# The gates of a scan in whole blocks of four products, woven four times into the projections

## The reference

```
gate_a = sigmoid(blockdiag(xr) @ wa[d] + ba[d])
gate_x = sigmoid(blockdiag(xr) @ wx[d] + bx[d])
log_a  = -8 * gate_a * softplus(-lam[d])
a, u   = exp(log_a), sqrt(-expm1(2 * log_a)) * gate_x * xr
h      = forward scan of (a[0], u[0]) + backward scan of (a[1], u[1])
y      = h * gelu(xg)
```

## Time and profile before

| | us |
|---|---|
| median of 3 runs (lowest, highest) | 1549.49 (1547.18, 1549.74) |
| the profiled execution | 1548.46 |
| its span, first to last instruction | 1546.6 |
| PE busy | 1457.9 |
| DVE busy | 1025.9 |
| ACT busy | 740.9 |
| POOL busy | 445.8 |

### The profile page before, as it was taken

The page is one execution under the profiler, slowest core; times in us unless marked ns, Lnnn a source line. Parts: engine busy times, 40 slices in busy tenths (PEclk is TensorE's granted clock), DMA queues, the critical chain, the costliest instruction groups (busy, mean ns, idle before and its releaser), DMA issues.

```text
span 1546.6 us, 16079 instructions
## 1 busy us (share of the span) xinstructions
PE 1457.9 (94%) x5958; PEld 1023.3 (66%) x5958; DVE 1025.9 (66%) x1032; ACT 740.9 (48%) x716; POOL 445.8 (29%) x225
## 2 busy tenths in 40 slices
PE   6999999999999999999999933999999999999997
PEld 3444487857675444555568832888888888888774
DVE  4533144473864655565545575998999999998896
ACT  3301001064633124455524431777777777777773
POOL 0031000000021007798963440222222233322204
PEclk9999999999999999999999965999999999999998
DMA  9311040030013000000223276999999999999994
GB/s 318 139 55 55 0 139 1 1 119 28 28 28 61 0 7 21 1 28 28 68 84 123 95 267 237 352 367 371 377 378 377 378 378 378 378 374 371 378 380 191
DMA packets 152887, 284.48 MB, mean 184 GB/s; under 512 B 25300, under 2 KB 35874, under 8 KB 152835
## 3 DMA queue, kind: packets, MB, share of 16 engines
q1 hardware_dynamic: 147219, 263.32, 47.8%
q0 software_dynamic: 4464, 16.25, 4.0%
q10 hardware_dynamic: 1152, 4.19, 0.7%
HBM read 259.10 MB, written 24.64 MB: 183 GB/s over the span
## 4 chain that ended last, share of the span: by engine, by line
PE 84%; DVE 6%; DMA 4%; ACT 2%; issue 2%; POOL 1%; SPq 0%; POOLq 0%; DVEq 0%; ACTq 0%
PE psum L1707 10%; PE psum L1709 10%; PE psum L1708 10%; PE psum L1249 7%; PE psum L1227 5%; PE psum L1480 4%; PE psum L1338 4%; PE psum L1209 4%; DMA arena<-in_exp_w_down 3%; PE psum L1542 3%; PE psum L1449 3%; PE psum L1174 2%; PE psum L1618 2%; PE psum L1620 2%; PE psum L1530 2%; PE psum L1619 2%
## 5 line engine op out<-in xcount | busy, mean ns | idle before, releaser
L2241 DVE TENSOR_TENSOR split_at<-arena,split_at 128x2048 fp32r<-128x2048 f32 x188 | 428.0, 2290 | 61.6 <-ACT split_at L1090 60.1
L1090 ACT ACTIVATE split_at<-arena 128x2048 fp32r<-128x2048 f32 x192 | 367.8, 1916 | 68.4 <-PE psum L1709 54.3
L1707 PE MATMUL psum<-split_at,split_at 128*128 128x512 f32 x768 | 306.4, 399 | 1.4 <-DVE split_at L2247 1.4
L1709 PE MATMUL psum<-split_at,split_at 128*128 128x512 f32 x768 | 300.6, 391 | 0.0
L1708 PE MATMUL psum<-split_at,split_at 128*128 128x512 f32 x768 | 300.0, 391 | 0.0
L1709 PEld LDWEIGHTS psum<-split_at,split_at 128*128 128x128 f32 x768 | 144.8, 189 | 31.3
L1707 PEld LDWEIGHTS psum<-split_at,split_at 128*128 128x128 f32 x768 | 145.0, 189 | 29.8 <-DVE split_at L2247 1.8
L1708 PEld LDWEIGHTS psum<-split_at,split_at 128*128 128x128 f32 x768 | 145.2, 189 | 28.4
L628 POOL TENSOR_TENSOR arena<-arena 128x1024 f32<-128x1024 f32 x48 | 114.1, 2376 | 122.1 <-ACT arena L972 119.6
L685 POOL COPY arena<-arena 128x1 uint32 (+1 forms) x14 | 28.3, 2020 | 360.7 <-DVE arena L2275 360.7
L2052 DVE TENSOR_REDUCE arena<-psum 128x1 f32<-128x1024 f32 x64 | 78.1, 1224 | 68.1 <-PE psum L1449 67.4
(11 more groups left out here) (313 smaller groups left out, 2477.9 us busy)
## 6 DMA issues: line engine op xcount, KB each, us to landing
arena<-in_exp_w_gate SPq DMA_DIRECT2D x64, 1024.0 KB, 14.3
arena<-in_exp_w_up SPq DMA_DIRECT2D x64, 1024.0 KB, 14.6
arena<-in_exp_w_down SPq DMA_DIRECT2D x64, 1024.0 KB, 14.3
arena<-in_w_in SPq DMA_DIRECT2D x9, 1024.0 KB, 7.9
arena<-in_x SPq DMA_DIRECT2D x8, 512.0 KB, 6.5
xhat_scratch<-arena SPq DMA_DIRECT2D x8, 512.0 KB, 10.0
arena<-in_w_out SPq DMA_DIRECT2D x8, 512.0 KB, 3.6
arena<-xhat_scratch SPq DMA_DIRECT2D x8, 512.0 KB, 5.0
```

What stands on the lines that cost most here:

```text
L1090: a(flat(wsplit[c % WS][0]), wraw[:, c], ACT.Copy).then_inc(s_whi, 1)
L1707: mm(bank(out_bank), src[0][:, k, :], whi[:, k % 4, :], start=(k == 0), stop=False)
L1709: ins = mm(bank(out_bank), src[1][:, k, :], whi[:, k % 4, :], start=False, stop=(k == KT - 1))
L2241: tt(flat(lo), wraw[:, c], flat(hi), ALU.subtract).then_inc(s_wlo, 1)
```

## The change

PE's `gates(q)` now computes both token halves in one block of four products: half 0 goes to banks 0 and 1 as before, half 1 to banks 2 and 3. It waits once, until ACT has read both halves of the block before. ACT reads half `j` from banks `2j` and `2j + 1` and always both halves in a row. The block stands at four places instead of eight: behind three units of `I_KV`, behind all of `I_KV`, behind all of `I_KV + 1`, and (block 3) behind nine units of `I_CQ + 1` and the wait for the rotated key, where its first half stood before. Block 2 thus lies whole ahead of `I_CQ`, where its halves lay behind 9 and behind 18 units of it. `sum_squares(0)`, which still follows 18 units of `I_CQ`, gets a wait for ACT's reads of block 2, because it writes banks 2 and 3. On ACT, the second half of block 2 moves ahead of the root of `ckv`, and the second half of block 3 ahead of the squares of `I_CQ + 1`.

```diff
@@ ACT
-            def gates(q, js=(0, 1)):
+            def gates(q):
...
-                for j in js:
+                for j in range(2):
                     act.wait_ge(s_gmm, 2 * q + j + 1)
                     h = slice(HALF * j, HALF * j + HALF)
-                    a(lx_[:, h], bank(1), ACT.Sigmoid, bias=par[:, C_BX + q:C_BX + q + 1])
-                    a(lt_[:, h], bank(0), ACT.Sigmoid, bias=par[:, C_BA + q:C_BA + q + 1]).then_inc(s_gact, 1)
+                    a(lx_[:, h], bank(2 * j + 1), ACT.Sigmoid, bias=par[:, C_BX + q:C_BX + q + 1])
+                    a(lt_[:, h], bank(2 * j), ACT.Sigmoid, bias=par[:, C_BA + q:C_BA + q + 1]).then_inc(s_gact, 1)
...
-            gates(2, (0,))
+            gates(2)
             rms_root(rb, 1, KVL)
-            gates(2, (1,))
             w_high(I_CQ + 2)
             squares(I_CQ, 2)
             w_high(I_CQ + 3)
             gate_rates(2)
-            gates(3, (0,))
+            gates(3)
             squares(I_CQ + 1, 3)
             w_high(I_CQ + 4)
-            gates(3, (1,))
             gate_rates(3)
@@ PE
-            def gates(q, j):
+            def gates(q):
...
-                if 2 * q + j:
-                    pe.wait_ge(s_gact, 2 * q + j)
-                for g in range(2):
-                    ins = mm(bank(g), lruw[:, 4 * d + 2 * g + c, :], xr[:, c, HALF * j:HALF * j + HALF], start=True, stop=True)
-                ins.then_inc(s_gmm, 1)
+                else:
+                    pe.wait_ge(s_gact, 2 * q)
+                for j in range(2):
+                    for g in range(2):
+                        ins = mm(bank(2 * j + g), lruw[:, 4 * d + 2 * g + c, :], xr[:, c, HALF * j:HALF * j + HALF], start=True, stop=True)
+                    ins.then_inc(s_gmm, 1)
 
             def sum_squares(n):
 
                 pe.wait_ge(s_sqa, (1, 6, 7)[n])
                 if n:
                     pe.wait_ge(s_rsd, n)
+                else:
+                    pe.wait_ge(s_gact, 6)
...
-            project_split(I_KV, 0, 9)
-            gates(0, 0)
-            project_split(I_KV, 9, 18)
-            gates(0, 1)
-            project_split(I_KV, 18, 24)
-            project_split(I_KV + 1, 0, 6)
-            gates(1, 0)
-            project_split(I_KV + 1, 6, 18)
-            gates(1, 1)
-            project_split(I_KV + 1, 18, 24)
-            project_split(I_CQ, 0, 9)
-            gates(2, 0)
-            project_split(I_CQ, 9, 18)
+            project_split(I_KV, 0, 3)
+            gates(0)
+            project_split(I_KV, 3, 24)
+            gates(1)
+            project_split(I_KV + 1)
+            gates(2)
+            project_split(I_CQ, 0, 18)
             sum_squares(0)
-            gates(2, 1)
             project_split(I_CQ, 18, 24)
             key_partners()
             project_split(I_CQ + 1, 0, 9)
             pe.wait_ge(s_kro, 1)
-            gates(3, 0)
+            gates(3)
             project_split(I_CQ + 1, 9, 24)
-            project_split(I_CQ + 2, 0, 9)
-            gates(3, 1)
-            project_split(I_CQ + 2, 9, 24)
+            project_split(I_CQ + 2)
```

More of the change, by code:

```diff
@@ L1375, in _ @@
             project_split(I_LG + 1)
-            def gates(q, j):
+            def gates(q):
                 d, c = divmod(q, 2)
-                if q == 0 and j == 0:
+                if q == 0:
                     pe.wait_ge(s_lw, 16 * 17)
```

## The result

The changed kernel takes 1550.59 us (median of 21 runs, 1548.38 to 1552.82), the kernel before 1548.54 (21 runs, 1546.63 to 1549.74). The ratio is 1.0014 with a 95% interval of 1.0008 to 1.0021: **2.0 us slower, between 1.2 and 3.3**. The forecast was +2.7.

What follows compares the result with a forecast made beforehand. PE, busy 94% of the span, was taken to bound the kernel, with a detour at the rotated key. +1.1 us of later restart and +1.6 of lower clock made +2.7 on 1549.49: 1552.2 us, range 1548.6 to 1554.2.

Steps and rivals of the forecast that it cites:

- PE bounds, with one detour at the rotated key: Stretch 320 to 500 us: PE, busy 94% of the span, sets the time, except for root, reciprocal and rotation on ACT and DVE.
- The sum of squares 1.61 later: First sum of squares on PE: issued at 401.95 instead of 400.34, as block 2 stands whole ahead of it.
- The chain of 15.70 us to the restart is strict: From issue of the sum of squares to PE's restart at the rotated key: 15.70 us unchanged, so restart at 417.65.
- The pause from 1.30 to 3.3: PE's idle time before the gates of block 3, waiting for the rotated key: grows from 1.30 to about 3.3 us.
- The wait at 448.64 goes, and +1.1 is left without the clock: PE's 0.24 us wait for DVE's bank read, with its restart about 0.4 us, disappears; +1.1 us carried to the end.
- The feared collision of DVE and POOL in block 3: A DVE scan meeting POOL's addition could put the bank read at 450.5 and cost 0.7 us, added to (a).
- The clock falls behind the pause, at 1.6 us: After PE's longer pause at the rotated key, 3.3 us of products at half speed; 1.6 us taken, ends 0 and 3.0.
- Rival (a): The longer pause at the rotated key without a fall of the clock: +1.1, 1550.6 us; chance 0.28.
- the rival of a lasting low level: Behind the pause at the rotated key the clock stays low for 6.1 us, 3.0 lost: +4.1, 1553.6 us; chance 0.16.
- the prediction's signs: Among them: the projection behind block 3's gates has products 0.43 apart instead of 0.23 for some 3 us.
- No part behind 490 changes: Stages behind 490 us shift only by the stretch's own amount; another shift would show the prediction wrong.
- rival (c): Block borders cost up to 0.30 us each instead of 0.05 and the clock stays high: +0.35, 1549.8 us; chance 0.10.

## Why the prediction was right

- **PE bounds, with one detour at the rotated key.** Right. Each kernel that moved the sum or filled the pause moved the stretch by what its PE timeline says.
- **The sum of squares 1.61 later.** 1.50 measured. The difference is the border of a whole block, 0.02 where I took 0.05, and ACT's and POOL's readiness was as described (square at 389.92, addition at 391.02, last gate read at 395.40).
- **The chain of 15.70 us to the restart is strict.** 417.04 - 401.33 = 15.71.
- **The pause from 1.30 to 3.3.** 3.18.
- **The wait at 448.64 goes, and +1.1 is left without the clock.** It went: DVE's read ended at 447.80, PE came at 450.88. ACT's slack for it was real: DVE waited 0.87 instead of 1.80 us. The stretch without the 1.71 of low clock is +0.92. The feared collision of DVE and POOL in block 3 didn't come: the step behind its first scan took 1.22 us (427.75), where the kernel before had one of 3.43 (426.76).
- **The clock falls behind the pause, at 1.6 us.** 1.71 measured between two kernels with the same products. Rival (a), a long pause without the fall, gives +1.1 and is excluded by the windows of this profile, and the rival of a lasting low level by the end of it at 421.2. The slow products weren't those of the projection, as the prediction's signs had it (0.43 apart): the clock fell 0.8 us behind the restart and rose at 421.2, so block 3 took all of it (5.40 instead of 3.59), and the projection from 421.87 on ran at full pace. At the rotated key, each kernel with a pause of 2.26 us or more had 0.50 behind it (three of three), each with one of 1.36 or less had 1.00 (three of three). The Trainium skill, "TensorE: Matmul & The Clock Gate", section "Why this matters for your kernels", advises against gaps between bursts of products above a length that is more than the 2.26 us here. The traces agree that a long gap is followed by the lower level, but 2.26 us was enough, and the measurement decides. That the fall came in this one profile of the changed kernel was foreseen; that it comes in each execution isn't shown.
- **No part behind 490 changes.** By the letter the prediction's sign of being wrong did appear: the heads begin 2.12 us later and the span is 4.0 us longer. But the 1.7 of it that came in the experts lies within what that stage scatters by in the ten profiles (2.1 us), so it speaks neither for nor against. The stretch gave +2.63, the runs gave +2.0 with an interval that holds it. That the forecast of +2.7 lies within 0.1 of the stretch is in part luck: its two terms were 0.2 too high and 0.1 too low.
- **Dearer borders, rival (c).** Excluded: four more borders cost 0.19 us in all.

What stays open: pauses between 1.36 and 2.26 us at the rotated key weren't tried, and what else besides the length of the pause enters, which the falls between 574 and 600 us show that something does.

## What to carry to other kernels

When products are gathered into larger blocks, ask first what stands behind them in PE's order: a short product that starts a chain on other engines (here 1.9 us of products that feed a root, a 6.5 us reciprocal and a rotation) must keep its place, or come as early as its inputs allow. The change saved 0.2 us of borders and put the sum 1.5 us later, which cost as much at the restart and 1.7 of lower clock behind it. But it also made the inputs of that chain ready 6 us sooner, and moving the sum to them turned 2.0 us slower into 1.1 to 2.3 us faster. A pause of PE is to be priced with the clock behind it: here, in one profile each, 0.9 us more of it (1.36 to 2.26) made the stretch 2.2 us longer. And before two profiles are compared, look for falls of the clock in the parts that the edit didn't touch.

## What the runs showed of the hardware

At the rotated key, pauses of 2.26, 3.18 and 4.13 us were each followed by the lower clock, and pauses of 1.30, 1.36 and 1.36 us weren't, nor was one of 1.77 us near 447 (PEclk 1.00 from 448 to 450). This is no general limit: the clock also fell behind a pause of 1.32 us in three of ten profiles and just behind one of 0.46 us in two, one of them of a kernel whose other profile stayed at 1.00 there, and it stayed high behind a pause of 2.02 us. Each of these falls lasted 3.4 us. At the rotated key one cost 1.7 us where it was measured, between 574 and 600 us one goes with 1.1 to 1.9 us more.

Going from full-precision products to rounded ones costs nothing in the block itself (from the start of a half-block to the second unit behind it are 2.18 us, where 1.717 and one unit of 0.453 make 2.17); it shows as a slower pace of the units behind it (0.46 to 0.47 instead of 0.453).
